# Mixture-of-experts weights in tiles of 256 rows by 1024 columns, two hidden slabs at a time

## What is computed

```python
def _swiglu(h, w_gate_up, w_down):          # D_MODEL = 1024, D_FF = 3584
    gu = h @ w_gate_up
    g, u = gu[..., :D_FF], gu[..., D_FF:]
    return (jax.nn.silu(g) * u) @ w_down
...
def _moe(h, router, w_gate_up, w_down):
    logits = (h @ router).astype(jnp.float32)
    top_v, top_i = lax.top_k(logits, TOP_K)
    gates = jax.nn.softmax(top_v, axis=-1)
...
    for e in range(N_EXPERTS):
        y = y + gate_full[..., e:e + 1] * _swiglu(h, w_gate_up[e], w_down[e])
    return y
```

## Time and profile before

| | us |
|---|---|
| median of 3 runs | 1589.36 |
| lowest, highest | 1588.41, 1589.93 |
| profiled execution | 1588.23 |
| its span, first to last instruction | 1586.2 |

### The profile page before, as it was taken

One profiled execution on the slowest core, in us unless ns is written; L12 is line 12 of the kernel. 1 busy time (PEld: TensorE's weight loads), 2 busy tenths in 40 slices (PEclk: granted clock), 3 DMA queues, 4 the chain that ended last, 5 costly groups with the idle time before them and its releaser, 6 DMA issues.

```text
span 1586.2 us, 19682 instructions
## 1 busy us (share of the span) xinstructions
PE 1496.4 (94%) x7570; PEld 1210.1 (76%) x7570; DVE 1178.2 (74%) x1008; ACT 1009.6 (64%) x861; POOL 139.7 (9%) x130
## 2 busy tenths in 40 slices
PE   8999999999999989999998999998999988999885
PEld 6888888899879967777775787776787766787663
DVE  5555544464655466998998888998988998888896
ACT  5453443343453366676887777887777887777784
POOL 0000000041305033100000000001000001000000
PEclk9999999999999999999999999999999999999998
DMA  9655555566427623999999999999999999999994
GB/s 337 215 169 183 179 185 186 186 194 209 155 84 228 197 78 108 378 360 375 365 388 381 384 387 388 377 388 382 383 388 382 381 388 383 383 388 370 390 387 168
DMA packets 238162, 469.38 MB, mean 296 GB/s; under 512 B 9792, under 2 KB 15936, under 8 KB 238064
## 3 DMA queue, kind: packets, MB, share of 16 engines
q1 hardware_dynamic: 231504, 453.93, 80.3%
q0 software_dynamic: 3072, 11.01, 2.3%
q10 hardware_dynamic: 3488, 3.13, 0.6%
HBM read 460.67 MB, written 7.37 MB: 295 GB/s over the span
## 4 chain that ended last, share of the span: by engine, by line
PE 66%; DMA 11%; DVE 9%; ACT 5%; SPq 5%; issue 3%; DVEq 0%; ACTq 0%
DMA raw<-in_m_w_gate_up_dram 8%; DVE wlo L320 6%; PE bY L337 6%; PE bY L339 6%; PE bY L338 6%; PE bG L337 5%; SPq L374 5%; PE bG L339 5%; PE bG L338 5%; PE bU L337 4%; PE bU L339 4%; PE bU L338 4%; ACT whi L314 4%; PE bS L339 3%; PE bS L337 3%; PE bS L338 3%
## 5 line engine op out<-in xcount | busy, mean ns | idle before, releaser
L320 DVE TENSOR_TENSOR wlo<-raw,whi 128x2048 fp32r<-128x2048 f32 x426 | 974.7, 2296 | 322.8 <-ACT whi L314 317.9
L314 ACT ACTIVATE whi<-raw 128x2048 fp32r<-128x2048 f32 x426 | 813.8, 1913 | 435.6 <-PE bS L339 132.9
L869 PE MATMUL bY<-whi,hTh 128*128 128x512 f32 x224 | 94.4, 422 | 24.7 <-DVE wlo L320 24.5
L869 PE MATMUL bG<-whi,eTh 128*128 128x512 f32 x224 | 92.8, 414 | 22.0 <-DVE wlo L320 21.9
L337 PE MATMUL bG<-whi,eTh 128*128 128x512 f32 x224 | 90.7, 405 | 6.5 <-DVE eTl L1314 3.7
L869 PE MATMUL bU<-whi,eTh 128*128 128x512 f32 x224 | 91.9, 410 | 4.4 <-DVE wlo L320 4.2
L337 PE MATMUL bU<-whi,eTh 128*128 128x512 f32 x224 | 91.2, 407 | 0.0
L870 PE MATMUL bY<-wlo,hTh 128*128 128x512 f32 x224 | 89.9, 402 | 0.0
L337 PE MATMUL bY<-whi,hTh 128*128 128x512 f32 x224 | 89.6, 400 | 0.0
L338 PE MATMUL bU<-whi,eTl 128*128 128x512 f32 x224 | 89.2, 398 | 0.0
L339 PE MATMUL bU<-wlo,eTh 128*128 128x512 f32 x224 | 89.2, 398 | 0.0
(11 more groups left out here) (439 smaller groups left out, 2946.6 us busy)
## 6 DMA issues: line engine op xcount, KB each, us to landing
raw<-in_m_w_gate_up_dram SPq DMA_DIRECT2D x224, 1024.0 KB, 13.9
raw<-in_m_w_down_dram SPq DMA_DIRECT2D x112, 1024.0 KB, 12.9
raw<-in_b_w_in_dram SPq DMA_DIRECT2D x36, 1024.0 KB, 5.2
raw<-in_f_w_gate_up_dram SPq DMA_DIRECT2D x28, 1024.0 KB, 5.2
raw<-in_f_w_down_dram SPq DMA_DIRECT2D x14, 1024.0 KB, 5.0
raw<-in_a_w_out_dram SPq DMA_DIRECT2D x4, 1024.0 KB, 15.7
biasrev<-toeplitz SPq DMA_DIRECT2D x32, 128.0 KB, 4.8
raw<-in_b_w_out_dram SPq DMA_DIRECT2D x4, 1024.0 KB, 5.0
```

The lines of the kernel that those rows point to most:

```text
L314: nc.scalar.activation(whi[:, t % CUT], raw[:, t % RAW], ACT.Copy).then_inc(hi_done, 1)
L320: nc.vector.tensor_tensor(wlo[:, t % CUT], raw[:, t % RAW], whi[:, t % CUT].bitcast(F32), ALU.subtract).then_inc(lo_done, 1)
L869: pe.matmul(backward(bank, 0, 512), xs[:, kb], w[0], start=kb == 0, stop=False)
```

## The change

The gate and up tiles of slabs 0 to 5 become 256 rows by 1024 columns: eight tiles hold gate and up of a pair of slabs, and a partition gets two pieces of 4 KB. Gate goes to G and S0, up to U and S1. Slab 6 keeps four 512 x 512 tiles (`SINGLE` = 24 is the first). Down tiles are 256 whole rows, two neighbouring rows per partition (one piece of 8 KB), which fill Y0 and Y1 together; so that the hidden units fit, the turn takes every second column. Item 7 (`by_half`) keeps 512-column down tiles. Slabs are turned in pairs, even ones in T and odd ones in Y1, which now has to be free before the first down tile. The two `y_out` copies of an item both come after its last tile. The gather of a half item fetches 64 rows instead of 128.

```diff
+        def expert_tile(gate_up, down, t, by_half):
+
+            if t < SINGLE:
+                g, r = divmod(t, 8)
+                part, q = divmod(r, 4)
+                c = part * FF + g * 1024
+                return gate_up[q * 256:q * 256 + 256, c:c + 1024].rearrange("(k p) n -> p k n", p=P)
+            if t < DOWN:
+                part, kh = divmod(t - SINGLE, 2)
+                c = part * FF + PAIRS * 1024
+                return gate_up[kh * 512:kh * 512 + 512, c:c + 512].rearrange("(k p) n -> p k n", p=P)
+            if by_half:
+                h, qn = divmod(t - DOWN, DT)
+                return down[qn * 512:qn * 512 + 512, h * 512:h * 512 + 512].rearrange("(k p) n -> p k n", p=P)
+            qn = t - DOWN
+            return down[qn * 256:qn * 256 + 256, :].rearrange("(p b) n -> p (b n)", b=2)
...
-                nc.gpsimd.indirect_dma_start(e_tok[:], None, hn_dram,
-                                             bass.IndirectOffsetOnAxis(from_rows[:, 0:1], 0)).then_inc(e_full, 16)
+                rows = slice(0, HALF_CAP if n % 2 == 0 else P)
+                nc.gpsimd.indirect_dma_start(e_tok[rows], None, hn_dram,
+                                             bass.IndirectOffsetOnAxis(from_rows[rows, 0:1], 0)).then_inc(e_full, 16)
...
+            def hidden_block(rows, c, by_half=False):
+
+                if by_half:
+                    return rows[:, c * P:c * P + P]
+                return rows.rearrange("p (i q b) -> p i b q", i=2, b=2)[:, c // 2, c % 2]
...
+            def full_item(n, k, amid=lambda g: None, late=lambda: None):
...
+                def turn(j):
+
+                    bank = (T, Y1)[j % 2]
+                    pe.wait_ge(h_ready, count(k, SLABS, PAIRS0 + j + 1))
+                    if j >= 2:
+                        pe.wait_ge(ht_lo, count(k, SLABS, PAIRS0 + j - 1))
+                    if j == 1 and n != 0:
+                        pe.wait_ge(y_hi, count(n, 2))
+                    for c in range(4):
+                        mm = pe.transpose(bank[:, c * P:c * P + P], hidden_block(up_rows(j), c), ident[:])
+                    mm.then_inc(ht_psum, 1)
...
+                for g in range(PAIRS):
+                    if g >= 1:
+                        pe.wait_ge(silu_done, count(k, SLABS, PAIRS0 + 2 * g))
+                    for q in range(4):
+                        if g == 0 and q == 2:
+                            third_wait(n)
+                        product(8 * g + q, eTh, eTl, (G, S0))
+                        if g >= 1 and q == 1:
+                            turn(2 * g - 2)
+                            turn(2 * g - 1)
+                    amid(g)
+                    for q in range(4):
+                        product(8 * g + 4 + q, eTh, eTl, (U, S1))
+                pe.wait_ge(silu_done, count(k, SLABS, PAIRS0 + 2 * PAIRS))
+                product(SINGLE, eTh, eTl, (G,))
+                turn(2 * PAIRS - 2)
+                turn(2 * PAIRS - 1)
+                product(SINGLE + 1, eTh, eTl, (G,))
+                amid(PAIRS)
+                product(SINGLE + 2, eTh, eTl, (U,))
+                product(SINGLE + 3, eTh, eTl, (U,))
+                pe.wait_ge(ht_lo, count(k, SLABS, PAIRS0 + 2 * PAIRS))
+                for qn in range(2 * DT):
+                    if qn == 2 * DT - 2:
+                        pe.wait_ge(ht_lo, count(k, SLABS, PAIRS0 + SLABS))
+                    product(DOWN + qn, hTh, hTl, (Y0, Y1))
+                    if qn == 1:
+                        turn(SLABS - 1)
+                    if qn == 10:
+                        late()
...
+            def half_item(n, k, amid=lambda g: None, late=lambda: None, by_half=False):
...
+                pe.wait_ge(jt_mul, count(k, SLABS, 2 * PAIRS))
+                for t in range(DOWN, FFN_TILES):
+                    slab = (t - DOWN) % DT if by_half else (t - DOWN) // 2
+                    if not by_half or t < DOWN + DT:
+                        pe.wait_ge(jt_lo, count(k, SLABS, slab + 1))
+                    product(t, hTh, (Y0, Y1))
+                    if t == DOWN + 1:
+                        turn(SLABS - 1)
...
+                ahead(SINGLE, SINGLE + 1)
+                hidden_hi(SLABS - 3)
+                silu(SLABS - 1)
+                hidden_hi(SLABS - 2)
+                ahead(SINGLE + 2, SINGLE + 3)
+                ahead(DOWN, DOWN + 1, DOWN + 2)
+                hidden_hi(SLABS - 1)
+                ahead(*range(DOWN + 3, DOWN + 12))
+                late()
+                ahead(DOWN + 12, DOWN + 13)
+                y_cut(0)
+                y_cut(1)
+
+            def half_item(n, k, y_cut, late=lambda: None, by_half=False, amid=lambda g: None):
+                def ahead(*tiles):
+                    for t in tiles:
...
+            def full_item(n, k, amid=lambda t: None, late=lambda: None, y_cut=lambda h: None, alone=False):
...
+                for g in range(PAIRS):
+                    t, a, b = 8 * g, 2 * g, 2 * g + 1
+                    ahead(t, t + 1, t + 2)
+                    if g >= 1:
+                        hidden_lo(a - 2)
+                    ahead(t + 3)
+                    if g >= 1:
+                        hidden_lo(a - 1)
+                    ahead(t + 4, t + 5, t + 6, t + 7)
+                    mul(a)
+                    mul(b)
+                ahead(SINGLE, SINGLE + 1)
+                hidden_lo(SLABS - 3)
+                ahead(SINGLE + 2)
+                hidden_lo(SLABS - 2)
+                ahead(SINGLE + 3)
+                mul(SLABS - 1)
+                ahead(DOWN, DOWN + 1, DOWN + 2)
+                hidden_lo(SLABS - 1)
+                ahead(*range(DOWN + 3, DOWN + 12))
+                late()
+                ahead(DOWN + 12, DOWN + 13)
+                y_cut(0)
+                y_cut(1)
...
+            def half_item(n, k, amid=lambda t: None, late=lambda: None, y_cut=lambda h: None, by_half=False):
...
+                for g in range(PAIRS):
+                    t, a = 8 * g, 2 * g
+                    ahead(t, t + 1, t + 2)
+                    if g >= 1:
+                        slab_mul(a - 2)
+                    ahead(t + 3)
+                    if g >= 1:
+                        slab_mul(a - 1)
+                    ahead(t + 4)
+                    if g >= 1:
+                        slab_lo(a - 2)
+                    ahead(t + 5)
+                    if g >= 1:
+                        slab_lo(a - 1)
+                    ahead(t + 6, t + 7)
+                ahead(SINGLE, SINGLE + 1)
+                slab_mul(SLABS - 3)
+                ahead(SINGLE + 2)
+                slab_mul(SLABS - 2)
+                slab_lo(SLABS - 3)
+                ahead(SINGLE + 3)
+                slab_lo(SLABS - 2)
+                ahead(DOWN, DOWN + 1, DOWN + 2, DOWN + 3)
+                slab_mul(SLABS - 1)
+                ahead(DOWN + 4, DOWN + 5)
+                slab_lo(SLABS - 1)
+                ahead(DOWN + 6)
+                if by_half:
+                    y_cut(0)
+                ahead(*range(DOWN + 7, DOWN + 12))
+                late()
+                ahead(DOWN + 12, DOWN + 13)
+                if by_half:
+                    y_cut(1)
...
+            aside = {1: gates_by_expert, 4: experts_by_load, 7: tables_by_slot, 10: table_of_rows, 13: full_experts,
+                     20: lambda: overflow(0), 22: lambda: overflow(1), 25: lambda: overflow(2), 27: lambda: overflow(3)}
```

More of the change, by code:

```diff
@@ L424, in _ @@
                 with sp.If(m < m_last):
-                    item_tiles((m, 1, E), expert(one((m, 1, E + 1))), range(FFN_TILES))
+                    e = expert(one((m, 1, E + 1)))
+                    for t in range(FFN_TILES):
+                        load_expert(t, (m, 1, E), e)
                 with sp.Else():
@@ L851, in full_item @@
-                for h in range(2):
-                    for qn, ks in enumerate(down):
-                        if h == 0:
-                            pe.wait_ge(ht_lo, count(k, SLABS, PAIRS0 + qn + 1))
-                        product(DOWN + DT * h + qn, hTh, hTl, ks, (Y0, Y1)[h], qn == DT - 1)
-                        if h == 0 and qn == 0:
-                            pe.wait_ge(ht_lo, count(k, SLABS, PAIRS0 + SLABS - 1))
-                            turn_hidden(SLABS - 1, 1, lambda tb: mh, count(k, SLABS, PAIRS0 + SLABS))
-                        if h == 1 and qn == 3:
-                            late()
@@ L1197, in full_item @@
[L1197 to L1211 removed]
+                    copy(hTh[:, 4 * j:4 * j + 4].rearrange("p c t -> p (c t)"), (T, Y1)[j % 2][:], ht_hi)
@@ L1688, in routed, with ahead @@
                 return dict(amid=amid, late=lambda: cut_next(n, half))
-            def full_item(n, k, amid=lambda j: None, late=lambda: None, y_cut=lambda h: None, alone=False, aside={}):
-                def ahead(t):
-                    if not alone or t + CUT < FFN_TILES:
-                        make_lo(dve, T_MOE + t + CUT, n)
```

(21 more changed lines are left out.)

430 lines of the change are left out of this document (220 added, 210 removed).

## The result

The changed kernel takes 1634.68 us (median of 4 runs, 1631.26 to 1635.50) against 1589.46 us for the kernel before: ratio 1.0281, 95% interval 1.0264 to 1.0299. I had forecast 1602.5, with 1580 to 1614 as the range. The direction was right, and the loss is 45 us instead of 13.

What follows compares the result with a forecast made beforehand. PE was taken to pace full items, DMA half items at 2.70 us a tile. Item 0 0, half items +0.4, full items +6.2, item 7 +2.6 and clock +4 gave +13.2, a median of 1602.5 us, range 1580 to 1614.

Steps and rivals of the forecast that it cites:

- the clock term: PE at 1.2 GHz after the new waits, eight of them at 1.7 us: bounds none and 13.6, taken as 4 us.
- the ring of the half items: Half items: chain of PE, ACT and DVE steps with two turns in a row, 22.1 us per eight tiles; item 112.0 us.
- the cut of slab 5: Full items: first down tile waits for `ht_lo` of slab 5, so PE stands 2.9 us in each; +6.2 us in items 2, 4, 6.
- the two products and two cuts in a row find cover: Full items: at 2.8 us of PE a tile these delay nothing, except before the first down tile; item 124.8 us.
- rival (4): A fall of the clock at each wait, 1612 us; forecast, this and rival (5) together had 0.73.
- item 0 at nothing: Item 0: the same 2.9 us wait, offset by finer routing work removing a 1.87 us wait and another microsecond; taken as 0.
- Item 7 at 2.6: Last item: tile 34 waits for slab 6's cut, now behind `wlo` of tile 36; 115.7 us against 113.05, +2.6.
- (1): Rival: transfers were the bound, half items fall to some 105.5 us, full items stay; 1563 us, chance 0.09.
- (5): Rival: strided turns are dear, up to 57 us; slower, outside the range; with forecast and rival (4) 0.73.
- (6): Rival: the 8 KB pieces are cut down, so the change does not do what it says; time as the forecast.
- (2): Rival: half way, half items at 110.0 us and the wait before the down tiles under 1 us; 1580 us, chance 0.10.
- (3): Rival: all cancels, full items' 2.9 us met by equal gains, within 3 us of 1589.4; chance 0.08.

Runs made afterwards that it cites:

- fill_waits: Changed kernel plus unneeded matmuls in PE's waits around the single slab of full items and before half items' first down tile: 1615.2 us.
- spread_turns: Changed kernel with full_order's and half_order's edits, and a pair's two turns in half items behind the second and third gate tiles: 1574.8 us.
- full_mul: Changed kernel with the two products of a pair of slabs moved ahead of one weight tile in DVE's part of full items: 1617.7 us.
- half_order: Changed kernel; in half items slab 5's product before the next weight tile's low cut, slab 6's product and cuts up to two weight tiles earlier: 1609.9 us.
- late_table: spread_turns with PE gathering the routing table's rows in item 0 one pair of slabs later: 1570.7 us, ratio 0.9885 to the kernel before.
- full_order: Changed kernel; in full items a pair's products and slab 5's low cut each moved ahead of one weight tile: 1602.0 us.
- pieces_2k_best: spread_turns with every expert tile loaded in 2 KiB pieces from 512 by 512 blocks (wrong weights, for times only): 1588.9 us.

## Why the prediction was right or wrong

Without the clock term the forecast was 9.2 us of loss; fill_waits, which has one of the 13 falls left, loses 25.7. With the clock it was 13.2, and the loss is 45.2. So both parts of the sum were too small, and the steps are these.

**Right: the ring of the half items.** Predicted 22.1 us per eight tiles; in item 5 of the changed kernel the tile behind the pair of turns starts at 1277.02 and then at 1299.32, 22.30 apart. PE's wait for `th` before the first down tile is 3.6 to 3.8 where I had 4.2. A half item without clock loss (fill_waits) is 113.1 against my 112.0. With the turns apart the ring is shorter but still there: in item 5 of spread_turns the turns of slabs 0 and 2 start at 1239.20 and 1260.93, 21.7 apart.

**Right: the cut of slab 5.** PE waits 2.43 us for `hTl` before the first down tile of item 4; I had 2.9. ACT hardly waits for `raw`, as forecast (0.8 us in all).

**Wrong: "PE has 2.8 us a tile, so the two products and two cuts in a row find cover ... One place has none."** There are two. In the pairs of slabs the turn comes after two gate tiles, and a product that stands behind one more `wlo` is ready by then. In the single slab it comes after one. I carried the rule from the pairs to the single slab without lining up its rows. The missed wait is 2.2 us long, costs 4.1 with its clock, and full_mul measured 17 us for it in the whole kernel. A full item came to 127.45 without the falls and to 130.5 with them, where I had 124.8.

**Wrong in size: the clock.** I took 4 us, with 0 and 13.6 as bounds, since the one wait of 1.81 us had brought one fall in four items and since half items would hide a part. It was 19.5 for twelve of the 13 stretches (fill_waits). In this kernel each of the 13 waits of 2.2 us and more brought a fall, the stretch at four of the five waits of 3.6 us and more is twice as long (6.8 us), and there were more waits than eight. Even my rival (4), a fall at each wait, stood at 1612 because it counted eight waits of one stretch each. That each such wait brings a fall is no rule, though. The kernel before has, in item 7, a longer wait than the one in the earlier trace rows, which I had not listed, and the 3.4 us behind it are at full clock (its row in the timeline, and that stretch, columns as in the earlier trace rows):

```profile
1481.24 0.50 PE L869 MATMUL bG<-whi,eTh 128*128 128x512 f32 x1 [3.02 <-DVE wlo L320]
1481.24:1484.65 3.41, 3.41 (x22) 3.05 (x22) 2.79 (x3) 2.60 (x3) 0.00 (x0) 1.00 1.06 388
```

The same 2.19 us ahead of the turn of slab 4 that brought a fall in each full item of the changed kernel brought none in item 4 of half_order (1185.41), which took 128.9 us where its items 2 and 6 took 130.9. From the start of item 0 on, the traces of this case have 14 waits of 1.8 to 2.0 us (8 with a fall), 33 of 2.2 to 3.0 (29 with one) and 26 of 3.6 and more (all with one, 15 of them of 6.8 us). Which of the shorter ones bring a fall stays open.

**Wrong: item 0 at nothing.** Item 0 lost 6.6: it has the waits of each full item (2.4 for `mbuf`, 2.7 for `hTl`, a fall at each), and a new one that I had not looked for, 2.0 us for the routing table, which is now asked for before it is ready. The wait of 1.87 us did go, as I expected, but I had let a vague gain from finer routing work cancel a cost that I had worked out. late_table took 4.0 us off spread_turns, where 3.4 us at half clock lie behind the wait for the table; in the changed kernel no fall lies there, so it costs less.

**Item 7 at 2.6: right in mechanism, the size is clock.** Tile 34 waits for slab 6, 5.2 us. The item's loss is 7.2 (136.5 against 129.3); in fill_waits, with one stretch of 6.8 us left in it (at most 3.4 us of loss), it is 4.5.

The sum, redone: full_order gives 32.7, nearly all in items 0, 2, 4, 6, where I had 6.2 before the clock; half_order gives 24.8, of which 10.9 in item 7; the pairs of turns 5.3; the table 4.0. These 66.8, less 2.9 that does not add, are the 63.9 between 1634.7 and 1570.7. Taking off the 18.7 us that the best kernel gains on the one before leaves the 45.2 that were lost.

**Rivals.** (1), transfers were the bound, was wrong for this kernel, but a gain of the larger pieces is there (14 us), once the waits are gone. It put half items at 105.5; the best ones are at 109.0. (5), strided turns up to 57 us, is out: 0.09 us a turn, 0.28 a pair. (6) is out: the page counts 12642 packets of 8 KB or more (151122 less 138480) where before it had 98 (238162 less 238064), and the 98 down tiles of items 0 to 6 are 12544 pieces of 8 KB. (2) and (3) did not occur.

**Left open:** why the half items stop at 109.0, with PE and DVE both idle for about 10 us of them, PE in short waits for `wlo` (the ring of 21.7 us per eight tiles is 2.7 us a tile, and no run shortens it further); and which waits under 3.6 us bring the clock down.

## What to carry to other kernels

Larger tiles thin out the order: a step that stood behind one small tile stands behind a large one, and what counts is not the average but each place where the pattern breaks off (the single slab, the start of the down tiles, the last item). Line up producer and consumer there, row by row, before judging the transfers. Here a wait of PE of 2.2 to 2.4 us cost 4.1 with the half clock that lay behind most of them (25 of 28), so put a price on the clock at each such wait, with a bound for a fall at every one. And a gain in bandwidth that seems not to exist may only be covered: put the waits right first, then measure it again.

## What the runs showed of the hardware

A wait of PE of 2.2 us was enough for a stretch of 3.4 us at 1.2 GHz (granted clock 0.50), and each of the 13 waits of that length and more in the changed kernel brought one; over all traces it was 29 of 33 waits of 2.2 to 3.0 us and 26 of 26 of 3.6 us and more, with a wait of 3.02 us that brought none. Falls came without any wait over 1.2 us too (four in pieces_2k_best). Matmuls whose result nobody uses, put into the waits, kept the clock at 2.4 GHz (1.00) and made the kernel 19.5 us faster. Loads of gate and up tiles in 4 KiB pieces ran at 410 GB/s where 2 KiB pieces ran at 387; in the down tiles 8 KiB pieces gave the same time as 2 KiB ones. A transpose that reads every second column of its data takes 280 to 283 ns instead of 272.
